# Eight of sixteen scale-and-add steps on the modulation row, moved from VectorE to POOL

## The chip, the cores and the metric

The kernel runs on one core of one Trainium2 chip. Its time is the device time of one execution in microseconds (us). TensorE is called PE here, ScalarE ACT, VectorE DVE, GpSimd POOL, and SyncE SP (in this kernel SP issues the weight loads). Each engine runs its own instruction list in order, and they meet at semaphores.

## The reference, cut to what matters

Two transformer-like blocks run one after the other on 256 tokens of width 2048, in float32. The change lies in the first block, where a condition vector `c` makes six modulation rows:

```
c_act = jax.nn.silu(c)
mod = c_act @ w_ada[l] + b_ada[l]
sh_m, sc_m, gt_m, sh_f, sc_f, gt_f = jnp.split(mod[:, None, :], N_MOD, axis=-1)
h = rmsnorm(x, pre_mix_norm[l]) * (1.0 + sc_m) + sh_m
proj = h @ w_in[l]
o_hg = hgrn2_group(proj[..., :HG_COLS], lb_all[l], hg_norm[l])
o_gdn = gdn_group(proj[..., HG_COLS:], gdn_conv_w[l], gdn_a_log[l], gdn_dt_bias[l], gdn_norm[l])
y = jnp.concatenate([o_hg, o_gdn], axis=-1) @ w_out[l]
x = x + gt_m * rmsnorm(y, post_mix_norm[l])
h = rmsnorm(x, pre_ffn_norm[l]) * (1.0 + sc_f) + sh_f
```

`sc_f` is the row of this change. It is a product of a vector of 2048 with 2048 columns of `w_ada`, and is first needed when `h` of the feed-forward is made. The two mixers, `hgrn2_group` (a decayed attention of 8 heads) and `gdn_group` (a gated delta rule with a triangular solve), stand between the projection `w_in` and the projection `w_out`.

## The kernel before

**Weights.** SP loads raw weights, 1 MB at a time (two k tiles of 128 rows by 1024 columns), into a ring of four slots, `raw_weights` (RAW). ACT rounds each k tile into `weights_high` (L351), DVE subtracts to get `weights_low` (L364), both in rings of four, and PE makes three products for each pair (L406 to L408). A load may start only when the user of the slot four loads before has said that it is done.

**The modulation rows.** `w_ada` goes through the same ring. A row of 2048 columns is summed in place, on all 128 partitions: for each k tile of 128 rows, `MOD = MOD + RAW * COLS[:, 112 + kt]`, where the last factor is one scalar of each partition. Later PE sums over the partitions with a matrix of ones (L1692). For `sc_f`, which lies in `MOD[:, 2, :]`, there are KT = 16 such steps, one 1 MB load each. Each is one DVE instruction on 128x2048 elements, recorded under L382 (`ada_step`, called by `ada_mix`). It counts up `ada_used`, on which the load four places later waits (L318). PE waits for all of them only in the first `w_out` chunk (`pe_mod2`, L1734). The first `w_out` chunk loads its first two pairs, then the sixteen `w_ada` tiles, then the rest.

**The mixers.** They run between the fourth k tile of the first `w_out` chunk and its fifth. Two programs are interleaved by hand, by strings of letters (L1521 to L1523): "h" is a step of the hgrn2 decay (class `Decay`), "g" one of the delta rule (`dve_delta`), "a" a modulation step, "n" the norm of the hgrn2 heads, "w" the weight of the delta rule's gate. In the DVE's list the order is:

1. Before the decay: two L364 of `w_out`, eight scalings (L1495), sixteen running sums along the tokens (L1503, a scan of 128x128 elements that has two SBUF inputs, the ones and the logs).
2. The decay, fourteen rounds of four instructions: two products (L992, L993), a difference (L985), and a masked copy of the scores from PSUM (L1001). At its end come two products (L1026, L1027).
3. The delta rule: the gram matrices (L1442 to L1455), then six levels of the triangular solve, each ended by two masked copies (L1461), then the addition L1464 and the outputs (L1467). The a, n and w steps stand between these.

**POOL.** It does little here. It clears a tile with a memset (L1548), then waits for the fifteenth decay (`decay_decays`) and copies the unit matrix twice into `XT` (L1551). The second gram step of DVE waits for that (`inverse_begun`). After that it makes two reciprocal roots (L621).

Of the kernel before, what the change touches and what calls it, by code (L numbers as in the profile page):

```python
# [11 lines left out]
F32 = mybir.dt.float32  # L12
F32R = mybir.dt.float32r
U8 = mybir.dt.uint8
ALU = mybir.AluOpType
# [127 lines left out]
def block_pair(nc, a, out, stop=None):  # L143

    with ExitStack() as ctx:
# [630 lines left out]
        def dve_first(dve):  # L776
# [32 lines left out]
            def input_low(q):  # L809
                k0, nk = GROUPS[q]  # L810
                for k in range(k0, k0 + nk):
                    dve.wait_ge(S("h_high"), k + 1)
                    dve.tensor_tensor(LL[:, k, :], XTURN[:, k, :], LH[:, k, :].bitcast(F32), ALU.subtract).then_inc(
                        S("h_low"), 1)

            dve.memset(STG[:, :, :], 0.0).then_inc(S("staged"), 1)
            dve.wait_ge(S("columns_ready"), 1)
# [552 lines left out]
        ADA_IN = 4 * KT  # L1370
        MIX_LOAD = MIX1.load_of(1) + 1

        def ada_mix(dve, first, count):

            for kt in range(first, first + count):
                m = MIX_LOAD + kt
                dve.wait_ge(S(f"weights_in{m % RAWN}"), 16 * (m // RAWN + 1))
                ada_step(dve, MOD[:, 2, :], RAW[:, m % RAWN, :, :].rearrange("p j n -> p (j n)"), kt, ADA_IN + kt)
# [104 lines left out]
                yield  # L1483

        def dve_ada_steps(dve):
            for kt in range(KT):
                ada_mix(dve, kt, 1)
                yield

# [30 lines left out]

        PE_PLAN = "g" + "h" * 6 + "g" + "h" * 14 + "g" * 4  # L1521
        ACT_PLAN = "hhh" + "g" + "hhh" + "g" + "h" * 12 + "g" + "r" + "gg" + "r" + "gg" + "r"
        DVE_PLAN = "hhhhg" + "h" * 27 + "g" + "aaa" + "ggg" + "a" + "nn" + "g" + "na" + "g" + "naa" + "gaaw" * 2 + "gaaa" + "gaa"  # L1523

        def dve_gdn_scale(dve):
            dve_rstd(dve, "gdn_heads", stat=STAT, n=DH)
# [19 lines left out]
        def pool_mix1(pool):  # L1546
            pool.wait_ge(S("hg_turned"), 1)
            pool.memset(PA[:, :, :], 0.0).then_inc(S("decay_cleared"), 1)  # L1548
            pool.wait_ge(S("decay_decays"), HG.TOTAL["decays"])
            for t in range(TT):  # L1550
                last = pool.tensor_copy(heads3(XT, t), IDENT.unsqueeze(1).to_broadcast([128, H1, 128]))  # L1551
            last.then_inc(S("inverse_begun"), 1)
            pool_rstd(pool, "hg_heads", STAT)
            pool_rstd(pool, "gdn_heads", STAT)
            pool.memset(MOD[:, 3, :], 0.0).then_inc(S("cleared"), 1)
            pool.wait_ge(S("cleared"), 2)
            pool.dma_start(MOD[0:1, 3, :], a["b_ada"][5 * D:6 * D].rearrange("(o n) -> o n", o=1)).then_inc(S("masks_in"), 16)
# [1223 lines left out]
```

## Time and profile before

| what | value |
|---|---|
| median of 3 runs | 2913.33 us (2912.28 to 2916.59) |
| span of the profiled execution | 2909.8 us |
| PE busy | 2702.3 us (93%) |
| DVE busy | 1819.0 us (63%) |
| ACT busy | 1224.1 us (42%) |
| POOL busy | 63.7 us (2%) |

The profile gives the span from the first to the last instruction of one execution. The median of the runs is 3.5 us above that span, and the profiled execution's own full time is not given apart from it. Busy shares are means over stages with different limits. In most of the program PE is what is waited for; the mixers, from about 476 us to about 645 us, are a stage of their own, and in it the share of the whole span says nothing.

In the rows further down a timeline's columns are: start in us, duration in us (of a merged group, from the start of its first to the end of its last), engine, line, operation, output<-inputs, how many, and in brackets the idle time before it with what ended it.

### The profile page before, as it was taken

To read this page: it belongs to the slowest core of one execution; us is meant where nothing else is said; L and a number is where in the kernel's file an instruction comes from. 1 tells how busy PE (TensorE), PEld (TensorE's weight loads), DVE (VectorE), ACT (ScalarE), POOL (GpSimd) and SP (SyncE) were. 2 spreads that over 40 slices of the span, in tenths; PEclk is the share of its full clock that TensorE was granted. 3 is DMA by queue.
4 is the path that set the end of the run, shared out by engine and by line. 5 is a ranking of instruction groups with operands and counts; after the bars stand their busy time and mean duration, and the time that the engine had idled before them with its cause. 6 is when DMAs were issued, how large, how long until landed. Compare 5 with 4: busy or idle time off the path is not lost.

```text
span 2909.8 us, 32548 instructions
## 1 busy us (share of the span) xinstructions
PE 2702.3 (93%) x12554; PEld 2188.7 (75%) x12554; DVE 1819.0 (63%) x2206; ACT 1224.1 (42%) x1560; POOL 63.7 (2%) x86
## 2 busy tenths in 40 slices
PE   4899998789799999999979999989999999999987
PEld 2378887687678888888767777877778887888876
DVE  7688677986865555555663556676455564646455
ACT  2134545333444444444444445444544434444333
POOL 1000000001000000000001000000000000000000
PEclk9899999999899999999989999999999999999998
DMA  9967885146575555555735443534345655465542
GB/s 377 338 213 268 289 313 192 58 174 249 209 259 185 186 188 190 187 185 187 259 117 199 148 141 131 187 118 173 132 172 175 201 174 195 167 201 174 165 154 100
DMA packets 154719, 562.29 MB, mean 193 GB/s; under 512 B 9688, under 2 KB 13943, under 8 KB 150768
## 3 DMA queue, kind: packets, MB, share of 16 engines
q1 hardware_dynamic: 150480, 542.15, 54.7%
q0 software_dynamic: 3952, 18.22, 1.8%
q8 instruction: 74, 1.21, 0.2%
q10 hardware_dynamic: 176, 0.40, 0.0%
q14 instruction: 37, 0.30, 0.0%
HBM read 556.28 MB, written 4.46 MB: 193 GB/s over the span
## 4 chain that ended last, share of the span: by engine, by line
PE 52%; issue 29%; DVE 12%; DMA 3%; ACT 3%; POOL 0%; DVEq 0%; SPq 0%; POOLq 0%; ACTq 0%
PE banks L406 15%; PE banks L408 15%; PE banks L407 15%; DMA raw_weights<-in_w_ada 3%; DVE weights_low L364 2%; ACT weights_high L351 2%; DVE mod_in L797 1%; PE banks L474 1%; DVE modulation L382 1%; PE banks L712 1%; DVE proj L1135 1%; DVE proj L1001 1%; PE banks L1692 0%; POOL small L621 0%; DVE proj L985 0%
## 5 line engine op out<-in xcount | busy, mean ns | idle before, releaser
L364 DVE TENSOR_TENSOR weights_low<-raw_weights,weights_high 128x1024 fp32r<-128x1024 f32 (+2 forms) x846 | 989.1, 1178 | 906.3 <-ACT weights_high L351 886.0
L351 ACT ACTIVATE weights_high<-raw_weights 128x1024 fp32r<-128x1024 f32 (+2 forms) x846 | 858.0, 1021 | 1018.2 <-PE banks L408 965.4
L406 PE MATMUL banks<-weights_high,lhs_high 128*128 128x512 f32 (+1 forms) x2208 | 883.7, 400 | 30.3 <-DVE weights_low L364 19.7
L408 PE MATMUL banks<-weights_high,lhs_low 128*128 128x512 f32 (+1 forms) x2208 | 865.4, 392 | 0.0
L407 PE MATMUL banks<-weights_low,lhs_high 128*128 128x512 f32 (+1 forms) x2208 | 864.6, 392 | 0.0
L406 PEld LDWEIGHTS banks<-weights_high,lhs_high 128*128 128x128 f32 x2208 | 420.1, 190 | 125.8 <-DVE weights_low L364 21.3
L408 PEld LDWEIGHTS banks<-weights_high,lhs_low 128*128 128x128 f32 x2208 | 419.5, 190 | 87.8
L407 PEld LDWEIGHTS banks<-weights_low,lhs_high 128*128 128x128 f32 x2208 | 420.5, 190 | 81.0 <-issue 1.0
L406 PE MATMUL banks<-weights_high,hid_high 128*128 128x512 f32 x856 | 337.5, 394 | 17.2 <-DVE hid_low L2563 6.4
L407 PE MATMUL banks<-weights_low,hid_high 128*128 128x512 f32 x856 | 335.2, 392 | 0.0
L408 PE MATMUL banks<-weights_high,hid_low 128*128 128x512 f32 x856 | 334.9, 391 | 0.0
L406 PEld LDWEIGHTS banks<-weights_high,hid_high 128*128 128x128 f32 x856 | 161.9, 189 | 57.4 <-DVE hid_low L2563 6.6
L408 PEld LDWEIGHTS banks<-weights_high,hid_low 128*128 128x128 f32 x856 | 162.0, 189 | 34.1
L407 PEld LDWEIGHTS banks<-weights_low,hid_high 128*128 128x128 f32 x856 | 162.1, 189 | 33.2 <-issue 0.2
L382 DVE SCALAR_TENSOR_TENSOR modulation<-raw_weights,columns,modulation 128x1024 f32<-128x1024 f32 (+1 forms) x112 | 160.6, 1434 | 2.6
L712 PE MATMUL banks<-first_weights,x_turned 128*128 128x512 f32 x192 | 93.6, 651 | 14.9 <-ACT x_turned L749 9.5
L797 DVE SCALAR_TENSOR_TENSOR mod_in<-raw_weights,columns,mod_in 128x512 f32<-128x512 f32 x120 | 89.1, 751 | 22.3 <-DMA raw_weights<-in_w_ada 18.2
L712 PEld LDWEIGHTS banks<-first_weights,x_turned 128*128 128x128 f32 x192 | 39.8, 211 | 65.7 <-issue 55.8
L2559 ACT ACTIVATE modulation<-modulation 128x512 f32<-128x512 f32 (+1 forms) x22 | 13.7, 622 | 107.9 <-DVE modulation L2586 107.9
L406 PE MATMUL banks<-weights_high,proj_turned 128*128 128x512 f32 x128 | 52.8, 413 | 4.2 <-DVE proj_turned L2232 2.5
L407 PE MATMUL banks<-weights_low,proj_turned 128*128 128x512 f32 x128 | 51.9, 406 | 0.0
L408 PE MATMUL banks<-weights_high,proj_turned 128*128 128x512 f32 x128 | 50.9, 398 | 0.0
(409 smaller groups left out, 2012.8 us busy)
## 6 DMA issues: line engine op xcount, KB each, us to landing
raw_weights<-in_w_ff SPq DMA_DIRECT2D x128, 1024.0 KB, 5.0
raw_weights<-in_w_ada SPq DMA_DIRECT2D x96, 1024.0 KB, 6.6
raw_weights<-in_w_in SPq DMA_DIRECT2D x96, 1024.0 KB, 5.4
raw_weights<-in_w_up SPq DMA_DIRECT2D x80, 1024.0 KB, 4.9
raw_weights<-in_w_down SPq DMA_DIRECT2D x42, 1024.0 KB, 5.1
raw_weights<-in_w_out SPq DMA_DIRECT2D x32, 1024.0 KB, 5.2
first_weights<-in_w_in SPq DMA_DIRECT2D x16, 768.0 KB, 12.6
raw_weights<-in_w_ckv SPq DMA_DIRECT2D x8, 1024.0 KB, 4.9
```

The lines of the kernel that those rows point to most:

```text
L351: act.activation(WHI[:, u % SPN, 0:c.width], RAW[:, n % RAWN, k % 2, 0:c.width], ACT.Copy).then_inc(S("high_made"), 1)
L364: dve.tensor_tensor(WLO[:, u % SPN, 0:c.width], RAW[:, n % RAWN, k % 2, 0:c.width], WHI[:, u % SPN, 0:c.width].bitcast(F32), ALU.subtract) ...
L382: dve.scalar_tensor_tensor(out=acc, in0=row, scalar=COLS[:, 112 + kt:113 + kt], in1=acc, op0=ALU.mult, op1=ALU.add).then_inc(S("ada_used"), 1)
L406: nc.tensor.matmul(o, x, hi, start=(k == 0), stop=False)
L407: nc.tensor.matmul(o, x, lo, start=False, stop=False)
L408: mm = nc.tensor.matmul(o, y, hi, start=False, stop=(k == c.kn - 1))
L474: tr = nc.tensor.transpose(bank[:, k, 128 * t:128 * t + 128], rows[:, t, c0:c0 + 128], IDENT)
L712: mm = nc.tensor.matmul(PS[:, bank, :], XTURN[:, k, 128 * t:128 * t + 128], raw[:, 512 * h:512 * h + 512], start=(k == 0), stop=(k == KT - 1))
L797: ins = dve.scalar_tensor_tensor(out=acc, in0=row, scalar=c, in1=acc, op0=ALU.mult, op1=ALU.add)
L1001: dve.copy_predicated(self.at[:, t, :].rearrange("p (h n) -> p h n", h=H), mask, self.slot(t).rearrange("p (h n) -> p h n", h=H)).then_inc ...
L1135: last = dve.scalar_tensor_tensor(out=dst, in0=src, scalar=w, in1=dst, op0=ALU.mult, op1=ALU.add)
L2559: act.activation(dst[:, 2 * q:2 * q + nk, :], GT[:, 2 * q:2 * q + nk, :], func).then_inc(S(done), 1)
```

## The change

POOL gets a function `pool_ada` with eight of the sixteen steps (kt 0 to 7). [...] POOL runs them after the memset and before the wait for the decays, and so before the two copies of the unit matrix. DVE keeps kt 8 to 15, and its order string is written anew. The count `h_low`, on which nothing waited, goes.

```
@@ -810,8 +810,7 @@
                 for k in range(k0, k0 + nk):
                     dve.wait_ge(S("h_high"), k + 1)
-                    dve.tensor_tensor(LL[:, k, :], XTURN[:, k, :], LH[:, k, :].bitcast(F32), ALU.subtract).then_inc(
-                        S("h_low"), 1)
+                    dve.tensor_tensor(LL[:, k, :], XTURN[:, k, :], LH[:, k, :].bitcast(F32), ALU.subtract)
@@ -1370,6 +1369,19 @@
         ADA_IN = 4 * KT
         MIX_LOAD = MIX1.load_of(1) + 1
 
+        POOL_STEPS = 8
+
+        def pool_ada(pool):
+
+            for kt in range(POOL_STEPS):
+                m = MIX_LOAD + kt
+                row = RAW[:, m % RAWN, :, :].rearrange("p j n -> p (j n)")
+                pool.wait_ge(S(f"weights_in{m % RAWN}"), 16 * (m // RAWN + 1))
+                pool.tensor_scalar(row, row, COLS[:, 112 + kt:113 + kt], None, ALU.mult).then_inc(S("row_scaled"), 1)
+                pool.wait_ge(S("row_scaled"), kt + 1)
+                pool.wait_ge(S("ada_used"), ADA_IN + kt)
+                pool.tensor_tensor(MOD[:, 2, :], MOD[:, 2, :], row, ALU.add).then_inc(S("ada_used"), 1)
+
@@ -1483,7 +1495,7 @@
         def dve_ada_steps(dve):
-            for kt in range(KT):
+            for kt in range(POOL_STEPS, KT):
                 ada_mix(dve, kt, 1)
                 yield
@@ -1520,7 +1532,7 @@
-        DVE_PLAN = "hhhhg" + "h" * 27 + "g" + "aaa" + "ggg" + "a" + "nn" + "g" + "na" + "g" + "naa" + "gaaw" * 2 + "gaaa" + "gaa"
+        DVE_PLAN = "hhhhg" + "h" * 27 + "gggg" + "nn" + "gn" * 2 + "gaw" * 2 + "gaaa" + "gaaa"
@@ -1546,6 +1558,7 @@
             pool.memset(PA[:, :, :], 0.0).then_inc(S("decay_cleared"), 1)
+            pool_ada(pool)
             pool.wait_ge(S("decay_decays"), HG.TOTAL["decays"])
```

Line numbers of the changed kernel are 12 or 13 higher in the mixers and 1 lower in the decay. Only two engines' lists differ. First POOL's, at the start of the mixers (`proj` is the tile that is cleared, `scratch` holds `XT`), in the kernel before:

```order
L1548 MEMSET proj 128x2x1024 [waits hg_turned]
L1551 COPY scratch<-tables 128x1024 [waits decay_decays]
L1551 COPY scratch<-tables 128x1024
L621 TENSOR_TENSOR small<-small 128x16 [waits mean_ready] x2
L1555 MEMSET modulation 128x2048
```

And in the changed kernel, the first three of the eight steps (the others are the same but for the slot):

```order
L1560 MEMSET proj 128x2x1024 [waits hg_turned]
L1380 TENSOR_SCALAR raw_weights<-raw_weights,columns 128x2048 [waits weights_in2]
L1383 TENSOR_TENSOR modulation<-modulation,raw_weights 128x2048 [waits ada_used,row_scaled]
L1380 TENSOR_SCALAR raw_weights<-raw_weights,columns 128x2048 [waits weights_in3]
L1383 TENSOR_TENSOR modulation<-modulation,raw_weights 128x2048 [waits ada_used,row_scaled]
L1380 TENSOR_SCALAR raw_weights<-raw_weights,columns 128x2048 [waits weights_in0]
L1383 TENSOR_TENSOR modulation<-modulation,raw_weights 128x2048 [waits ada_used,row_scaled]
```

Sixteen instructions of 128x2048 now stand between the memset and the copies.

Then DVE's list from the gram matrices to the first level of the solve, before:

```order
L1442 SCALAR_TENSOR_TENSOR scratch<-banks,modulation 128x1024
L1445 COPY_PREDICATED scratch<-masks,scratch 128x1024
L382 SCALAR_TENSOR_TENSOR modulation<-raw_weights,columns,modulation 128x2048 x3
L1442 SCALAR_TENSOR_TENSOR scratch<-banks,modulation 128x1024
L1445 COPY_PREDICATED scratch<-masks,scratch 128x1024
L1449 TENSOR_TENSOR modulation<-modulation,banks 128x1024 x2
L1452 SCALAR_TENSOR_TENSOR scratch<-banks,scratch 128x1024
L1455 TENSOR_TENSOR scratch<-scratch,banks 128x1024
L382 SCALAR_TENSOR_TENSOR modulation<-raw_weights,columns,modulation 128x2048
```

In the changed kernel:

```order
L1454 SCALAR_TENSOR_TENSOR scratch<-banks,modulation 128x1024
L1457 COPY_PREDICATED scratch<-masks,scratch 128x1024
L1454 SCALAR_TENSOR_TENSOR scratch<-banks,modulation 128x1024
L1457 COPY_PREDICATED scratch<-masks,scratch 128x1024
L1461 TENSOR_TENSOR modulation<-modulation,banks 128x1024 x2
L1464 SCALAR_TENSOR_TENSOR scratch<-banks,scratch 128x1024
L1467 TENSOR_TENSOR scratch<-scratch,banks 128x1024
```

All four modulation steps of that piece are gone. Last, DVE's list from the third level of the solve to the addition behind the sixth, before:

```order
L1461 COPY_PREDICATED proj<-masks,banks 128x1024 x2
L382 SCALAR_TENSOR_TENSOR modulation<-raw_weights,columns,modulation 128x2048 x2
L1481 TENSOR_TENSOR proj<-proj,small_rows 128x1024
L1461 COPY_PREDICATED proj<-masks,banks 128x1024 x2
L382 SCALAR_TENSOR_TENSOR modulation<-raw_weights,columns,modulation 128x2048 x2
L1481 TENSOR_TENSOR proj<-proj,small_rows 128x1024
L1461 COPY_PREDICATED proj<-masks,banks 128x1024 x2
L382 SCALAR_TENSOR_TENSOR modulation<-raw_weights,columns,modulation 128x2048 x3
L1461 COPY_PREDICATED scratch<-masks,banks 128x1024 x2
L382 SCALAR_TENSOR_TENSOR modulation<-raw_weights,columns,modulation 128x2048 x2
L1464 TENSOR_TENSOR proj<-proj,banks 128x1024
```

In the changed kernel:

```order
L1473 COPY_PREDICATED proj<-masks,banks 128x1024 x2
L382 SCALAR_TENSOR_TENSOR modulation<-raw_weights,columns,modulation 128x2048
L1493 TENSOR_TENSOR proj<-proj,small_rows 128x1024
L1473 COPY_PREDICATED proj<-masks,banks 128x1024 x2
L382 SCALAR_TENSOR_TENSOR modulation<-raw_weights,columns,modulation 128x2048
L1493 TENSOR_TENSOR proj<-proj,small_rows 128x1024
L1473 COPY_PREDICATED proj<-masks,banks 128x1024 x2
L382 SCALAR_TENSOR_TENSOR modulation<-raw_weights,columns,modulation 128x2048 x3
L1473 COPY_PREDICATED scratch<-masks,banks 128x1024 x2
L382 SCALAR_TENSOR_TENSOR modulation<-raw_weights,columns,modulation 128x2048 x3
L1476 TENSOR_TENSOR proj<-proj,banks 128x1024
```

Two levels have one step less, and behind the last level there is one more than before, three instead of two, ahead of the addition.

## Rows read from the trace of the kernel before

**Rows 1.** Busy time by stretch (us: PE, PEld, DVE, ACT, POOL; clock, DMA share, GB/s).

```profile
486.00:548.00 62.00, 36.85 (x273) 34.02 (x273) 60.67 (x64) 23.23 (x46) 3.01 (x2) 0.92 0.00 1
...
588.00:633.00 45.00, 40.57 (x351) 38.89 (x349) 41.00 (x25) 17.40 (x17) 0.00 (x0) 1.00 0.66 246
```

**Rows 2.** The chain of waits, 440 to 700 us: start, us, what.

```profile
480.48 5.17 DVE scratch L1503 x16
...
632.76 1.23 DVE proj L1464
```

**Rows 3.** DVE timeline, one round of the decay.

```profile
510.00 0.69 DVE L992 TENSOR_TENSOR proj<-proj,scratch 128x512 f32<-128x512 f32 x1
510.61 0.69 DVE L993 TENSOR_TENSOR scratch<-scratch 128x512 f32<-128x512 f32 x1
511.21 1.22 DVE L985 TENSOR_TENSOR proj<-scratch 128x1024 f32<-128x1024 f32 x1
512.34 1.30 DVE L1001 COPY_PREDICATED proj<-masks,banks 128x1024 f32<-128x1024 uint8 x1
```

**Rows 4.** Timeline of DVE and POOL at the end of the decay.

```profile
540.37 1.22 DVE L1019 TENSOR_TENSOR scratch<-scratch 128x1024 f32<-128x1024 f32 x1
...
543.71 3.01 POOL L1551 COPY scratch<-tables 128x1024 f32<-128x1024 f32 x2 [85.97 <-ACT proj L971]
543.88 1.95 DVE L1026 TENSOR_TENSOR scratch<-scratch 128x1024 f32<-128x1024 f32 x1
545.75 2.05 DVE L1027 TENSOR_TENSOR proj<-proj,scratch 128x1024 f32<-128x1024 f32 x1
```

**Rows 5.** The two POOL copies by themselves: duration in ns, least/median/most.

```profile
L1551 POOL COPY scratch<-tables x2: 1033/1528/2024, 543.7 to 544.7; 128x1024 f32<-128x1024 f32 x2
```

**Rows 6.** POOL's memset, and DVE beside it, timelines.

```profile
455.94 1.81 POOL L1548 MEMSET proj<- 128x2048 f32 x1 [350.92 <-PE banks L1150]
...
456.46 2.60 DVE L382 SCALAR_TENSOR_TENSOR modulation<-raw_weights,columns,modulation 128x1024 f32<-128x1024 f32 x2
```

**Rows 7.** POOL timeline: a two-input instruction, a power.

```profile
576.28 2.94 POOL L621 TENSOR_TENSOR small<-small 128x16 f32<-128x16 f32 x1 [29.56 <-DVE small L1040]
```

**Rows 8.** SP's issue of the first tile, and issues 455 to 640 us (last: us to landing).

```profile
463.79 0.34 SPq L320 DMA_DIRECT2D raw_weights<-in_w_ada  x1
...
raw_weights<-in_w_ada SPq DMA_DIRECT2D x16, 1024.0 KB, 5.0
```

**Rows 9.** DVE timeline ahead of the decay.

```profile
470.69 1.23 DVE L364 TENSOR_TENSOR weights_low<-raw_weights,weights_high 128x1024 fp32r<-128x1024 f32 x1 [1.50 <-ACT weights_high L351]
473.83 1.23 DVE L364 TENSOR_TENSOR weights_low<-raw_weights,weights_high 128x1024 fp32r<-128x1024 f32 x1 [1.92 <-ACT weights_high L351]
477.02 2.67 DVE L1495 TENSOR_SCALAR scratch<-scratch,small,columns 128x256 f32<-128x256 f32 x8 [1.97 <-ACT scratch L1354]
480.48 5.16 DVE L1503 TENSOR_TENSOR_SCAN scratch<-tables,scratch 128x128 f32<-128x128 f32 x16 [0.78 <-ACT scratch L1358]
```

**Rows 10.** DVE timeline, modulation steps in the delta rule and what waits beside them.

```profile
550.16 7.25 DVE L382 SCALAR_TENSOR_TENSOR modulation<-raw_weights,columns,modulation 128x2048 f32<-128x2048 f32 x3
560.26 1.22 DVE L1442 SCALAR_TENSOR_TENSOR scratch<-banks,modulation 128x1024 f32<-128x1024 f32 x1 [2.85 <-PE banks L1240]
...
568.99 2.34 DVE L382 SCALAR_TENSOR_TENSOR modulation<-raw_weights,columns,modulation 128x2048 f32<-128x2048 f32 x1
...
583.99 2.35 DVE L382 SCALAR_TENSOR_TENSOR modulation<-raw_weights,columns,modulation 128x2048 f32<-128x2048 f32 x1
...
627.35 4.79 DVE L382 SCALAR_TENSOR_TENSOR modulation<-raw_weights,columns,modulation 128x2048 f32<-128x2048 f32 x2
632.76 1.22 DVE L1464 TENSOR_TENSOR proj<-proj,banks 128x1024 f32<-128x1024 f32 x1 [0.62 <-PE banks L1279]
```

**Rows 11.** PE timeline in the solve, and ACT's first weight tile behind the mixers.

```profile
587.61 2.28 PE L1272 MATMUL banks<-tables,proj 128*128 128x128 f32 x16 [0.52 <-DVE proj L1461]
...
647.98 1.06 ACT L351 ACTIVATE weights_high<-raw_weights 128x1024 fp32r<-128x1024 f32 x1 [2.44 <-PE banks L408]
```

## The prediction

> **What bounds the kernel now.** I read the busy time by stretch first. From 486 to 548 us, the decay, DVE is busy 60.67 of 62 us; in the solve, 588 to 633 us, PE (40.57 of 45) and DVE (41.00) are both near full [rows 1]. The chain of waits then says which of them is waited for. It runs through DVE's sixteen scans at 480.48, and much later through the addition L1464 at 632.76 [rows 2]. DVE's timeline shows the decay as a closed row: L992, L993, L985 and L1001 start 0.61, 0.60 and 1.13 us apart, and the round ends at 513.64, 3.64 us after it began [rows 3]. No idle time stands in it. So the reader should see two regimes. Up to 548 us whatever delays DVE delays the end, one for one. Behind that the modulation steps on DVE fill time in which it would mostly wait for PE.
>
> The change takes work out of the second regime and puts work on POOL beside the first. The question is whether POOL's work is free there.
>
> **Does POOL hold DVE up?** The trace has one place where POOL reads SBUF while DVE does the same. L1019, a DVE instruction of 128x1024 with two SBUF inputs, takes 1.22 us alone. L1026 and L1027, of the same size and kind, take 1.95 and 2.05 us, and beside them run POOL's two copies [rows 4]. The first copy takes 1033 ns, from 543.71 to 544.74; the second, from 544.70, takes 2024 [rows 5]. Laid on one line: L1026 starts at 543.88 and ends at 545.83, which is 1.09 behind the end of copy 1. Copy 2 ends at 546.72, 0.89 behind the end of L1026. L1027 ends at 547.80, 1.08 behind the end of copy 2. That isn't two engines slowing each other a little. It is strict turns: each waits for the other's whole instruction, and the one that has waited goes next. DVE lost 0.73 + 0.83 us.
>
> The other place shows what doesn't collide: while POOL's memset of 2048 elements runs (455.94 to 457.75), two DVE steps L382 of 128x1024, also with two SBUF inputs, take 2.60 us together [rows 6]. Held to the memset's end they would have ended at 460.2 and not at 459.06. A memset reads nothing.
>
> The Trainium skill has the rule (SBUF — State Buffer, "Who interferes with whom"): a DVE instruction with two SBUF inputs contends with a GpSimd instruction that reads SBUF but not with one that only writes, and the loser blocks for the whole instruction. The trace agrees in both halves, by the 1.95 and 2.05 us and by the memset. It speaks against this change: both of POOL's new instructions read SBUF.
>
> **What a POOL step costs.** No row has POOL scaling or adding. Scaling reads one tile, as the copy does: 1.03 us for 1024 elements [rows 5], so 2.0 for 2048; memset's 1.81 [rows 6] is the end below. The addition reads two tiles. Its low end is the copy's rate, 2.0. If both inputs come through the door for which the copy took turns, it is twice that, 4.0. The only two-input row is a power, 2.94 us for 16 elements [rows 7], which by its rate would make 376 us of 2048; the power itself must cost that, since a copy goes through 1024 elements in 1.03, so it is no price of an addition. For a slow software loop I keep half as much again as high end, 3.0 and 6.0. I take 2.0 and 4.0, 6.0 us of held door per step.
>
> The Trainium skill (GPSIMD Engine Reference, section 3.1) has a measured 4497 ns for an fp32 tensor_tensor of 2048 elements. With it the total below would be 3.3 us more, about 2957 us. No run here shows it yet.
>
> **When, and beside what.** POOL is free from 457.75. The first tile's load is issued at 463.79 and takes 5.0 us to land [rows 8], so POOL starts at about 469 to 469.5. The next tiles come ahead of need: a slot is given back at each addition's end, its load takes 5.0, and it is wanted three steps, 18 us, later. From there, in turns with DVE [rows 9]:
> - Scaling 0 from 469.5 to 471.5; the L364 due at 470.69 (1.14 us) goes next; addition 0 from 472.6 to 476.6, and the L364 of 473.83 is pushed to 477.8. The eight scalings L1495 read one tile (2.67 us), run freely, and end near 480.5, when the scans start anyway. Cost so far nothing.
> - Scaling 1 follows that L364, 477.8 to 479.8, and addition 1 runs from 480.1 to 484.1. The scans, due at 480.48, have two SBUF inputs: 3.6 us lost.
> - Six steps are left, twelve instructions. Between each two goes one scan of 0.32 us (5.16/16). DVE loses 6 x 6.0 = 36.0 us.
>
> The sum is 39.6 us, and the scans stretch from 5.2 to about 45. POOL is done at about 524, before the decay is, so the fourteen rounds then run at 3.64 us again, and POOL's copies still come in time for `inverse_begun`. PE and ACT only wait longer. DVE is the chain there, so nothing gives this back.
>
> **What DVE gains and loses later.** The three steps at 550.16 (7.25 us) go, but DVE idled 2.85 us behind them for a PE product [rows 10]: worth nothing. The steps at 568.99 and 583.99 stand ahead of L1461 of the first two levels; the row of PE behind the second shows 0.52 idle on L1461 [rows 11], so I take 0.5 us gained, where 0 and 4.7 (both steps in full) are the ends. In the levels after that, PE's products of one level hide one or two steps. Behind the sixth level there are now three steps, not two: 627.35 plus 7.2 (the three at 550.16 took 7.25) is 634.5, but L1464 was wanted and started at 632.76, after 0.62 idle [rows 10], and is on the chain [rows 2]. That is 1.7 us lost. The last tiles of `w_out` are loaded up to 2.5 us later; ACT took the first of them at 647.98 after waiting for PE, not for a load [rows 11]: nothing. The missing count `h_low` costs nothing, since no one waits for it.
>
> **The sum.** +39.6 - 0.5 + 1.7 = +40.8 us. The profiled span was 2909.8; 2950.6 is the span after. The median of the runs stands 3.5 us above the span, so 2954 us.
>
> **The rivals.**
> 1. *The scans don't take turns*, only the products do. For it: no row shows a scan beside a reading POOL. Against: it has two SBUF inputs as L1026 has. POOL then runs three more instructions freely, and in the decay 1.2 us of L1001 (which reads PSUM and the masks) hides part of each third instruction: played through in the same way, 26 us lost, 2941 us. An addition at the copy's rate gives 24 us, 2938. I call both the small case, 2930 to 2946.
> 2. *POOL is slow.* With 3.0 and 6.0 us a step is 9.0: 6 x 9.0 plus 6 ahead, +60, 2974 us; above 2968 I count this case. If POOL is so slow or so often last that it ends after 543.7, the delay shows at L1551 and L1442 instead, of the same size.
> 3. *Not slower: POOL's work passes beside DVE's*, as the memset did [rows 6]. This would be so if only copies from the constant tables collide, or if POOL's two-input loop lets DVE in between elements. It is decided at L992 and L985: if they stay at 0.69 and 1.22 beside POOL, the price is zero. Then only the late terms are left: +1.2, or 2914.5 us; with both early steps on the chain in full, 4.7 - 1.7 = 3.0 gained, 2910. Against it stand L1026 and L1027. A form between, where DVE loses 6 to 16 us, gives 2920 to 2930.
> 4. *The relief counts for more than I read.* DVE sheds eight steps of 2.34 us [rows 10], 18.7 in all, and some of it might shorten levels that look bound by PE. Beside a POOL that collides with nothing, that is the only way to be faster. PE's 40.57 of 45 us [rows 1] leaves at most 4 us there, so 2906.
>
> **How the numbers follow.** Forecast, 2946 to 2968: 0.58. Small case: 0.16. Slow POOL: 0.11. Between, 2920 to 2930: 0.05. Nothing held, 2910 to 2919: 0.06. Relief: 0.04. What a measurement can tell from no change is about 0.2%, 5.8 us. Slower is 0.58 + 0.16 + 0.11 + 0.05 = 0.90; same 0.06; faster 0.04. The range from 2930 to 2980 takes in the forecast, the small case and most of the slow one, and leaves out 0.15 below and about 0.05 above.
>
> **What would show it.** Right: the group of scans takes about 45 us instead of 5.16, in pieces between POOL's instructions; POOL's sixteen instructions end near 524; rounds of the decay behind that keep 3.64 us; the decay's end moves from 547.80 to about 587; L1464 (now L1476) starts with no idle before it, and the distance from L1027's end to it grows from 85.0 to about 86.2 us. Wrong: two-input DVE instructions beside POOL at their old lengths, scans at 0.32 us each while POOL adds, or a gram step that waits for POOL's copies.

## The result, and the profile after

| what | before | changed |
|---|---|---|
| median in one comparison | 2914.96 us (2912.28 to 2917.97, 4 runs) | 2971.25 us (2970.3 to 2973.13, 4 runs) |
| span of the profiled execution | 2909.8 us | 2969.7 us |
| DVE busy | 1819.0 us | 1863.3 us |
| POOL busy | 63.7 us | 145.5 us |

The ratio is 1.0189 [1.0175, 1.0203]: slower by 56.3 us. The forecast was 2954, so the direction was right and the size 17 us too small: the result lies inside the stated range of 2930 to 2980, but above the 2946 to 2968 of the forecast, in the case of a slow POOL. DVE gave eight instructions of 2.34 us away and is busy for 44 us more, which by itself says that something else holds it.

The kernel after, timelines of POOL and of DVE at the start of the mixers (start, us, engine, line, what).

```profile
457.38 1.81 POOL L1560 MEMSET proj<- 128x2048 f32 x1 [352.08 <-PE banks L1149]
471.36 5.45 POOL L1380 TENSOR_SCALAR raw_weights<-raw_weights,columns 128x2048 f32<-128x2048 f32 x1 [12.17 <-DMA raw_weights<-in_w_ada]
476.90 4.77 POOL L1383 TENSOR_TENSOR modulation<-modulation,raw_weights 128x2048 f32<-128x2048 f32 x1
481.66 5.47 POOL L1380 TENSOR_SCALAR raw_weights<-raw_weights,columns 128x2048 f32<-128x2048 f32 x1
487.21 4.49 POOL L1383 TENSOR_TENSOR modulation<-modulation,raw_weights 128x2048 f32<-128x2048 f32 x1
...
548.78 4.88 POOL L1383 TENSOR_TENSOR modulation<-modulation,raw_weights 128x2048 f32<-128x2048 f32 x1
602.23 3.01 POOL L1564 COPY scratch<-tables 128x1024 f32<-128x1024 f32 x2 [48.57 <-ACT proj L970]
```

```profile
472.13 5.16 DVE L364 TENSOR_TENSOR weights_low<-raw_weights,weights_high 128x1024 fp32r<-128x1024 f32 x2 [1.49 <-ACT weights_high L351]
478.46 38.89 DVE L1507 TENSOR_SCALAR scratch<-scratch,small,columns 128x256 f32<-128x256 f32 x8 [1.17 <-ACT scratch L1353]
517.39 20.61 DVE L1515 TENSOR_TENSOR_SCAN scratch<-tables,scratch 128x128 f32<-128x128 f32 x16
538.13 0.06 DVE L1519 MEMSET small<- 128x1 f32 x1
538.13 5.26 DVE L984 TENSOR_TENSOR proj<-scratch 128x1024 f32<-128x1024 f32 x1
...
604.26 2.05 DVE L1026 TENSOR_TENSOR proj<-proj,scratch 128x1024 f32<-128x1024 f32 x1
```

The line numbers shift: the decay's L992, L993, L985 and L1001 are now L991, L992, L984 and L1000, and the last two products L1026 and L1027 are now L1025 and L1026. Against [rows 9] and [rows 4] the reader sees three places. The eight scalings (L1495 before, L1507 now) take 38.89 us instead of 2.67, the sixteen scans 20.61 instead of 5.16, and the products of the decay are held until POOL ends at 553.66. The next views put their durations side by side (ns: least, median, most); the first row is of the kernel before.

```profile
L1495 DVE TENSOR_SCALAR scratch<-scratch,small,columns x8: 407/408/412, 477.0 to 479.3; 128x256 f32<-128x256 f32 x8
```

```profile
L1507 DVE TENSOR_SCALAR scratch<-scratch,small,columns x8: 3358/5092/5528, 478.5 to 511.8; 128x256 f32<-128x256 f32 x8
L1515 DVE TENSOR_TENSOR_SCAN scratch<-tables,scratch x16: 391/393/4676, 517.4 to 537.6; 128x128 f32<-128x128 f32 x16
L1380 POOL TENSOR_SCALAR raw_weights<-raw_weights,columns x8: 5448/5474/6410, 471.4 to 542.3; 128x2048 f32<-128x2048 f32 x8
L1383 POOL TENSOR_TENSOR modulation<-modulation,raw_weights x8: 4492/4568/4881, 476.9 to 548.8; 128x2048 f32<-128x2048 f32 x8
```

A POOL step is 5.47 + 4.49 = 10.0 us where the forecast had 2.0 + 4.0. Exactly eight POOL instructions, the addition at 476.90 to the scaling at 511.73, stand beside the eight scalings of DVE: one of DVE's goes between each two, in strict turns.

The windows show who waits for it (columns as in [rows 1]).

```profile
478.00:538.00 60.00, 7.17 (x48) 7.01 (x48) 59.50 (x24) 8.79 (x12) 59.50 (x13) 0.56 0.36 123
538.00:606.00 68.00, 41.08 (x272) 38.26 (x272) 67.50 (x64) 23.30 (x46) 18.59 (x5) 0.85 0.09 31
606.00:621.00 15.00, 13.43 (x85) 13.16 (x86) 3.10 (x4) 5.02 (x11) 0.00 (x0) 0.69 0.00 1
```

From 478 to 538 us DVE and POOL are both busy all the time, with 24 DVE instructions that need 7.83 us between them in [rows 9], and PE has 7.17 us of work. Nothing fills this stretch, so it is added to the span.

The loss in pieces, each as the distance between two starts after, less the same before: from the first scaling to the first scan 38.93 - 3.46 = 35.5 us, over the scans 20.74 - 5.29 = 15.4, over the decay 66.13 - 59.98 = 6.2. That is 57.1 us, where the forecast had 39.6, all of it at the scans. The border between scans and decay is a DVE memset; in the kernel before it is this row:

```profile
485.77 0.06 DVE L1507 MEMSET small<- 128x1 f32 x1
```

Outside the 57.1 us, the first scaling starts 1.4 us later than before (478.46 and 477.02); POOL's memset, ahead of POOL's new work, starts 1.44 later too. That is no effect of the change: in another trace, of a kernel whose list is the same as before up to there (the last experiment), that memset starts at 457.18, 1.24 later. The rest is in the delta rule, below.

### The profile page after: what moved, and what is told of

Same layout as the page of the kernel before. It is cut to its first block, busy times and chain, and to the rows that moved or that the text cites. A ratio compares the mean times of both kernels' runs of the same rounds, so it can differ in the third digit from the quotient of the medians.

```text
span 2969.7 us, 32557 instructions
## 1 busy us (share of the span) xinstructions
PE 2712.1 (91%) x12554; PEld 2198.2 (74%) x12554; DVE 1863.3 (63%) x2198; ACT 1224.3 (41%) x1560; POOL 145.5 (5%) x102
## 4 chain that ended last, share of the span: by engine, by line
PE 52%; issue 28%; DVE 13%; ACT 3%; DMA 3%; POOL 0%; SPq 0%; DVEq 0%; POOLq 0%; ACTq 0%
PE banks L406 15%; PE banks L408 15%; PE banks L407 15%; DMA raw_weights<-in_w_ada 3%; DVE weights_low L364 2%; ACT weights_high L351 2%; DVE mod_in L797 1%; DVE scratch L1507 1%; PE banks L712 1%; DVE modulation L382 1%; PE banks L474 1%; DVE scratch L1515 1%; DVE proj L1134 1%; DVE proj L984 1%; PE banks L1264 1%
## 5 line engine op out<-in xcount | busy, mean ns | idle before, releaser
L382 DVE SCALAR_TENSOR_TENSOR modulation<-raw_weights,columns,modulation 128x1024 f32<-128x1024 f32 (+1 forms) x104 | 141.8, 1364 | 2.1
L621 POOL TENSOR_TENSOR small<-small 128x1 f32<-128x1 f32 (+3 forms) x17 | 15.9, 935 | 1254.3 <-DVE small L606 1009.2
L406 PE MATMUL banks<-weights_high,proj_turned 128*128 128x512 f32 x128 | 52.8, 413 | 4.2 <-DVE proj_turned L2245 2.5
L928 PE MATMUL banks<-scratch 128*128 128x128 f32 x32 | 6.4, 391 | 52.5 <-DVE small L1519 52.5
## 6 DMA issues: line engine op xcount, KB each, us to landing
first_weights<-in_w_in SPq DMA_DIRECT2D x16, 768.0 KB, 12.6
```

Of the source, the lines that this page charges most:

```text
L382: dve.scalar_tensor_tensor(out=acc, in0=row, scalar=COLS[:, 112 + kt:113 + kt], in1=acc, op0=ALU.mult, op1=ALU.add).then_inc(S("ada_used"), 1)
L406: nc.tensor.matmul(o, x, hi, start=(k == 0), stop=False)
```

## The experiments

Diffs are against the changed kernel. The time of the profiled execution stands about 1.8 us above its span here. A time with a ratio is a median of 4 to 10 runs; one without is a single run, and single runs of the kernel before lie between 2909 and 2919 us, so a few us between two such times say nothing. A steadier measure, which also leaves out what comes behind the decay, is the start of the decay's last instruction (L1026; L1027 in the kernel before), counted from the start of POOL's memset ahead of the mixers. In the kernel before and in the three kernels that have no such work on POOL ahead of L1026 it agrees within 0.05 us.

| kernel | POOL's memset | L1026 | distance | above the kernel before |
|---|---|---|---|---|
| before | 455.94 | 545.75 | 89.81 | |
| changed | 457.38 | 604.26 | 146.88 | 57.1 |
| count only | 457.84 | 547.68 | 89.84 | 0.0 |
| additions only | 456.48 | 576.01 | 119.53 | 29.7 |
| four steps on POOL | 457.77 | 578.51 | 120.74 | 30.9 |
| only writes on POOL | 458.18 | 560.61 | 102.43 | 12.6 |
| DVE's scalings by constants | 457.32 | 598.73 | 141.41 | 51.6 |
| POOL scales by a constant | 458.52 | 604.04 | 145.52 | 55.7 |
| POOL scales by a repeated column | 456.80 | 602.38 | 145.58 | 55.8 |
| POOL's steps behind the scans | 455.68 | 598.73 | 143.05 | 53.2 |
| the same, repeated column | 456.61 | 597.11 | 140.50 | 50.7 |
| the same, copy | 457.04 | 585.71 | 128.67 | 38.9 |
| three steps, behind POOL's copies | 456.95 | 546.81 | 89.86 | 0.0 |
| four of DVE's steps in the gap | 457.18 | 547.02 | 89.84 | 0.0 |

**Count only.** POOL's steps are left out; a memset of one column does the counting. The eight steps' part of the sum is missing.

```
-                pool.tensor_scalar(row, row, COLS[:, 112 + kt:113 + kt], None, ALU.mult).then_inc(S("row_scaled"), 1)
-                pool.wait_ge(S("row_scaled"), kt + 1)
                 pool.wait_ge(S("ada_used"), ADA_IN + kt)
-                pool.tensor_tensor(MOD[:, 2, :], MOD[:, 2, :], row, ALU.add).then_inc(S("ada_used"), 1)
+                pool.memset(SM[:, 220:221], 0.0).then_inc(S("ada_used"), 1)
```

> Leaves POOL's eight scalings and eight additions out (a one-column memset counts in their place), and keeps DVE's new order. Turns theory (DVE waits for POOL's whole instructions): nothing of that is left, only the late terms of the order, +1.2 us, so 2914 to 2918. Rival (the new DVE order or later loads cost much by themselves): well above, 2930 or more.

Measured: 2916.39 us, ratio 1.0006 [0.9996, 1.0015]. L1026 starts as far behind the memset as in the kernel before. So the whole loss comes from what POOL executes; eight steps fewer on DVE, in another order, give nothing that the runs can tell. This also takes the rival of the relief away.

**Additions only.** The scaling is left out.

```
-                pool.tensor_scalar(row, row, COLS[:, 112 + kt:113 + kt], None, ALU.mult).then_inc(S("row_scaled"), 1)
-                pool.wait_ge(S("row_scaled"), kt + 1)
```

> Leaves the scaling out; POOL only adds the raw tile. Turns theory: POOL's addition stays 4.5 us, the loss is the sum of POOL's instructions from 478.5 us on, some 2.5 + 6 x 4.5 = 30 us, plus 1.2: about 2945. Rival (the loss goes by the number of collisions or by something else than the length): it would stay near 2971, or halve its 57 to about 2943; the row of one DVE scaling beside an addition tells these apart (4.6 us each under turns).

Measured: 2939.54 us, below both 2943 and 2945, so the time alone does not part them; the scalings do, with 4662 ns in the median against the 4.6 us of the turns theory. DVE's timeline of this kernel:

```profile
480.65 28.30 DVE L1505 TENSOR_SCALAR scratch<-scratch,small,columns 128x256 f32<-128x256 f32 x8
508.98 5.16 DVE L1513 TENSOR_TENSOR_SCAN scratch<-tables,scratch 128x128 f32<-128x128 f32 x16
```

The scans are untouched, since POOL is done at 508.8 us. The scalings pay most: 28.30 us for 2.67 us of work. Of the 29.7 us, 24.9 lie between the first scaling and the first scan. Another 3.1 lie ahead of them, and 1.8 in the decay, where the first masked copy waits 2.78 us for PE instead of 1.05 (PE's granted clock was 0.73 in the first 15 us of the decay, 0.91 in the kernel before).

**Four steps on POOL.** DVE has the other twelve, in an order close to that of the kernel before.

```
-        POOL_STEPS = 8
+        POOL_STEPS = 4
-        DVE_PLAN = "hhhhg" + "h" * 27 + "gggg" + "nn" + "gn" * 2 + "gaw" * 2 + "gaaa" + "gaaa"
+        DVE_PLAN = "hhhhg" + "h" * 27 + "gggg" + "a" + "nn" + "g" + "na" + "g" + "na" + "gaaw" * 2 + "gaaa" + "gaa"
```

> POOL does four steps, DVE twelve. Turns theory: four steps of 10 us less on DVE's path, so 57 - 40 = 17 us lost and about 2932. Rival (a fixed cost of having POOL at work there, or of the clock): more than half of the 57 stays, 2943 or more.

Measured: 2941.61 us, just under the rival's 2943 and 10 us above the forecast. DVE's timeline:

```profile
478.86 32.98 DVE L1507 TENSOR_SCALAR scratch<-scratch,small,columns 128x256 f32<-128x256 f32 x8 [1.97 <-ACT scratch L1353]
511.87 5.16 DVE L1515 TENSOR_TENSOR_SCAN scratch<-tables,scratch 128x128 f32<-128x128 f32 x16
```

Half the steps cost about half (30.9 of 57.1 us), so a fixed cost is not what one sees. Nearly all of it, 29.6 us, is paid by eight instructions that in the prediction ran free. My expectation took off 10 us for each step left out. The four that are left out are the ones that fall beside the scans and the decay, where a step costs less, as a later experiment shows.

**Only writes on POOL.** Each of the sixteen instructions becomes a memset of the raw tile; the sums are left out.

```
-                pool.tensor_scalar(row, row, COLS[:, 112 + kt:113 + kt], None, ALU.mult).then_inc(S("row_scaled"), 1)
+                pool.memset(row, 0.0).then_inc(S("row_scaled"), 1)
-                pool.tensor_tensor(MOD[:, 2, :], MOD[:, 2, :], row, ALU.add).then_inc(S("ada_used"), 1)
+                pool.memset(row, 0.0).then_inc(S("ada_used"), 1)
```

> Each of POOL's sixteen instructions is replaced by a memset of the same tile (1.81 us), which only writes; the eight steps' sums are left out. If only POOL's reads collide, neither scalings nor scans are held: 2915. If an instruction of DVE that uses both ports for one tile also needs POOL's write side, the eight scalings take about 1.8 to 2 us each beside the memsets and the scans stay at 0.32: about 8 x 1.8 = 14 us more, 2929.

Measured: 2925.46 us, nearest to the second of the two cases. The durations of the scalings, then the times of the two engines:

```profile
L1507 DVE TENSOR_SCALAR scratch<-scratch,small,columns x8: 1258/1966/1971, 479.3 to 491.8; 128x256 f32<-128x256 f32 x8
```

```profile
479.27 14.48 DVE L1507 TENSOR_SCALAR scratch<-scratch,small,columns 128x256 f32<-128x256 f32 x8 [1.97 <-ACT scratch L1353]
493.79 5.16 DVE L1515 TENSOR_TENSOR_SCAN scratch<-tables,scratch 128x128 f32<-128x128 f32 x16
```

```profile
493.55 1.95 POOL L1380 MEMSET raw_weights<- 128x2048 f32 x1
495.55 1.80 POOL L1383 MEMSET raw_weights<- 128x2048 f32 x1
```

The two kinds of DVE instruction part here. A scaling with one SBUF input is held by a mere write, from 0.41 to 1.97 us. The scans, with two SBUF inputs, run beside POOL's memsets at their old length (5.16 us for the sixteen), as L382 did in [rows 6]. The Trainium skill (SBUF — State Buffer, "Who interferes with whom") says why the first can be: tensor_scalar may enter a mode that uses both port pairs, its own and the one shared with GpSimd. In the prediction I weighed the sentence of that section on two-input instructions and passed over this one; this run agrees with it, by the 1.97 us.

**DVE's scalings by constants.** The two scalars of each partition become -0.5 and 0.5.

```
-                last = dve.tensor_scalar(Lb[1][:, :, hs], Lb[2][:, :, hs], LB_LESS_1[:, h:h + 1], COLS[:, 104 + h:105 + h],
+                last = dve.tensor_scalar(Lb[1][:, :, hs], Lb[2][:, :, hs], -0.5, 0.5,
```

> The eight DVE scalings ahead of the scans take constants and not two scalars per partition. If the scalars' reads made them wait for POOL, they now take 0.4 us each beside POOL, and the scans take the turns in their place, so the time stays within 3 us of 2971. If they wait because the instruction uses both ports for its one tile, they still take about 5 us each; time 2971 as well.

Measured: 2968.21 us. The eight take 18.60 us and not 38.89, the longest of them 5449 ns, about a whole scaling of POOL:

```profile
L1507 DVE TENSOR_SCALAR scratch<-scratch x8: 273/1425/5449, 478.4 to 496.7; 128x256 f32<-128x256 f32 x8
497.04 20.53 DVE L1515 TENSOR_TENSOR_SCAN scratch<-tables,scratch 128x128 f32<-128x128 f32 x16
```

Neither forecast fits. Four of the eight are still held (2.57, 5.45, 4.58 and 5.45 us), so the reading of scalars is not what holds them; but behind each of these one passes in about 0.3 us. So here DVE does two instructions between two of POOL's, and not one. Why is open. Of the 20 us saved here all but 5.5 come back, since POOL's other steps then fall beside the decay.

**POOL scales by a constant.** In POOL's scaling the scalar of each partition becomes 0.5.

```
-                pool.tensor_scalar(row, row, COLS[:, 112 + kt:113 + kt], None, ALU.mult).then_inc(S("row_scaled"), 1)
+                pool.tensor_scalar(row, row, 0.5, None, ALU.mult).then_inc(S("row_scaled"), 1)
```

> The scaling is by the constant 0.5 and not by the condition's column. If the scalar read for each partition makes it 5.47 us, it falls to about 2.0 and the time to about 2971 - 7 x 3.5 = 2947. If POOL's tensor_scalar is slow whatever the scalar, 5.4 us and 2971.

Measured: 2973.55 us, the second case; POOL's scaling takes 5435 ns in the median, against 5474. The scalar's source is not the price.

**POOL scales by a repeated column.** The scaling becomes a multiplication of two tiles, one of which is the column repeated.

```
-                pool.tensor_scalar(row, row, COLS[:, 112 + kt:113 + kt], None, ALU.mult).then_inc(S("row_scaled"), 1)
+                pool.tensor_tensor(row, row, COLS[:, 112 + kt:113 + kt].to_broadcast([128, 2 * UW]), ALU.mult).then_inc(
+                    S("row_scaled"), 1)
```

> The scaling is made by tensor_tensor with the scalar's column repeated along the tile, as two inputs. If POOL's tensor_scalar of 5.47 us is slow because of its own code, this one costs 4.5 like the addition: seven steps of 1.0 us less, 2964. If every multiplication costs 5.4 on POOL, no change, 2971.

Measured: 2970.73 us, ratio 1.0192 [1.0175, 1.0209]. That is the time of the rival, but not for its reason, since the multiplication does not cost 5.4 us. The scaling is shorter by a third and the kernel no faster:

```profile
L1380 POOL TENSOR_TENSOR raw_weights<-raw_weights,columns x8: 3646/3680/4578, 469.5 to 529.0; 128x2048 f32<-128x2048 f32 x8
512.80 27.91 DVE L1516 TENSOR_TENSOR_SCAN scratch<-tables,scratch 128x128 f32<-128x128 f32 x16
```

What the scalings of DVE save (32.79 us instead of 38.89) the scans pay (27.91 instead of 20.61). That asked for a finer look at what of POOL's scaling holds DVE.

**POOL's steps behind the scans.** POOL waits for the memset that ends the scans, so all its steps fall on the decay.

```
             pool.memset(PA[:, :, :], 0.0).then_inc(S("decay_cleared"), 1)
+            pool.wait_ge(S("decay_inputs"), 1)
             pool_ada(pool)
```

> POOL's steps wait until the scans are done and run beside the decay rounds only. Turns theory: sixteen instructions of 80 us in all, one DVE instruction with two SBUF inputs between each two, hidden only behind the masked copies (1.2 us of each third): about +74 in the decay, 2990. Rival (POOL slows DVE in proportion to its traffic, wherever it runs): the same 57 as before, 2971.

Measured: 2969.34 us. My expectation of 2990 was 21 us too high, and the rival's 2971 was right in the number. The round of the decay tells why. DVE, then POOL:

```profile
504.04 4.49 DVE L991 TENSOR_TENSOR proj<-proj,scratch 128x512 f32<-128x512 f32 x1
508.45 0.68 DVE L992 TENSOR_TENSOR scratch<-scratch 128x512 f32<-128x512 f32 x1
509.06 4.65 DVE L984 TENSOR_TENSOR proj<-scratch 128x1024 f32<-128x1024 f32 x1
513.63 1.30 DVE L1000 COPY_PREDICATED proj<-masks,banks 128x1024 f32<-128x1024 uint8 x1
515.00 4.49 DVE L991 TENSOR_TENSOR proj<-proj,scratch 128x512 f32<-128x512 f32 x1
```

```profile
503.48 4.50 POOL L1383 TENSOR_TENSOR modulation<-modulation,raw_weights 128x2048 f32<-128x2048 f32 x1
507.96 6.40 POOL L1380 TENSOR_SCALAR raw_weights<-raw_weights,columns 128x2048 f32<-128x2048 f32 x1
514.44 4.51 POOL L1383 TENSOR_TENSOR modulation<-modulation,raw_weights 128x2048 f32<-128x2048 f32 x1
```

One POOL step goes with one round of DVE, 10.96 us from 504.04 to 515.00 instead of the 3.64 of [rows 3]: 7.3 us lost per step. The addition costs L991 4.49 - 0.69 = 3.8. POOL's scaling costs L984 only 4.65 - 1.22 = 3.4, and it still runs for 0.65 us after L984 has ended at 513.71. L984 needs 1.22 us, so it was let in at about 512.5, some 1.9 us before the scaling's end at 514.36. The masked copy, with its data in PSUM, keeps 1.30. L992 keeps 0.68: it passes while the scaling has only begun, and the scaling in turn takes 6.40 us here and not 5.47. So the rival's reason fails: a POOL that slowed DVE in proportion to its traffic would stretch all four instructions.

The theory from this: POOL's tensor_scalar of 5.47 us holds a two-input DVE instruction for some 3.6 us, and not for a tail of about 1.8, in which it might only write, since a memset of the same tile takes 1.81. The scans of the changed kernel agree: one scan beside an addition, but many beside the end of a scaling (two answers of its timeline on DVE, each a stretch of one POOL instruction).

```profile
527.67 4.65 DVE L1515 TENSOR_TENSOR_SCAN scratch<-tables,scratch 128x128 f32<-128x128 f32 x1
532.24 5.44 DVE L1515 TENSOR_TENSOR_SCAN scratch<-tables,scratch 128x128 f32<-128x128 f32 x6
```

Two runs test it at the place where all of DVE's held instructions have two SBUF inputs. Both are the kernel with POOL's steps behind the scans, with another instruction in place of POOL's scaling. **The repeated column, behind the scans:**

```
-                pool.tensor_scalar(row, row, COLS[:, 112 + kt:113 + kt], None, ALU.mult).then_inc(S("row_scaled"), 1)
+                pool.tensor_tensor(row, row, COLS[:, 112 + kt:113 + kt].to_broadcast([128, 2 * UW]), ALU.mult).then_inc(
+                    S("row_scaled"), 1)
```

> As the run in which POOL's eight steps start behind the fill of decay_inputs (2969.3 us), and POOL's scaling is made by a multiplication with the repeated column, which took 3.65 us where it stood alone in place of 5.47. Theory, refined: only the part of a POOL instruction in which it still reads holds VectorE's instructions of two SBUF inputs; the scaling by tensor_scalar reads for about 3.65 us and only writes for the last 1.8. Then the shorter form gains nothing: it holds (3.65 + 4.5) x 8 = 65 us, less what falls beside the masked copies, 53 to 59 us lost, 2968 to 2975 us. Rival, POOL's instruction holds VectorE for its whole length: 8 steps get shorter by 1.8 to 2.7 us, 14 to 22 us in all, 2948 to 2955 us.

Measured: 2966.85 us. Against the kernel with tensor_scalar there, L1026 comes 143.05 - 140.50 = 2.5 us sooner, or 0.3 per step. The theory had none, and the rival 14 to 22. **A copy in place of the scaling, behind the scans** (the scaling is left out):

```
-                pool.tensor_scalar(row, row, COLS[:, 112 + kt:113 + kt], None, ALU.mult).then_inc(S("row_scaled"), 1)
+                pool.tensor_copy(row, row).then_inc(S("row_scaled"), 1)
```

> As the run in which POOL's eight steps start behind the fill of decay_inputs (2969.3 us), with the scaling left out and a copy of the raw row onto itself in its place, which by the copies of 128x1024 at 1.03 us takes about 2.0 us. Theory, refined (what POOL reads holds VectorE): (2.0 + 4.5) x 8 = 52 us, less some 6 beside masked copies, about 46 us lost, 2961 us. Rival, whole length: POOL's step falls from 10.96 to about 6.5 us, 8 x 4.4 = 35 us less than 2969, 2934 us.

Measured: 2953.19 us, L1026 at 585.71. The forecast of 2961 was 8 us too high and the rival's 2934 19 us too low. The difference to the tensor_scalar there is 143.05 - 128.67 = 14.4 us, or 1.8 per step. A tensor_scalar that holds for 3.65 and a copy that holds for 2.0 differ by 1.65; their whole lengths differ by about 3.5. The theory is the nearer one, not exact.

```profile
L1380 POOL TENSOR_TENSOR raw_weights<-raw_weights,columns x8: 4042/4048/4587, 486.6 to 551.7; 128x2048 f32<-128x2048 f32 x8
```

```profile
L1380 POOL COPY raw_weights<-raw_weights x8: 2337/2607/2888, 487.0 to 539.0; 128x2048 f32<-128x2048 f32 x8
```

(The first row is of the run with the column, the second of the run with the copy; both hold waits for DVE.) The tail of about 1.8 us shows in three places: at L984 here, at the scans, and at a masked copy in the next run. That it is a phase of writing is argued, not shown: from the memset's length, and from DVE's scalings, which a memset holds and which are also held to the end of POOL's scaling (5.1 to 5.5 us).

**Three steps, behind POOL's copies.** POOL makes three steps, where DVE waits for PE.

```
-        POOL_STEPS = 8
+        POOL_STEPS = 3
-        DVE_PLAN = "hhhhg" + "h" * 27 + "gggg" + "nn" + "gn" * 2 + "gaw" * 2 + "gaaa" + "gaaa"
+        DVE_PLAN = "hhhhg" + "h" * 27 + "gggg" + "nn" + "gna" + "gnaa" + "gaaa" + "gaaw" + "gaaa" + "gaaw"
-            pool_ada(pool)
             pool.wait_ge(S("decay_decays"), HG.TOTAL["decays"])
...
             last.then_inc(S("inverse_begun"), 1)
+            pool_ada(pool)
```

> POOL does three steps, behind its two copies of the unit matrix (about 547 to 577 us), where most of DVE's instructions read PSUM and DVE waits for PE; DVE does thirteen. Turns theory: held are only the masked copy from SBUF (L1457) and the two products of the hgrn2 heads, up to 5 us each and partly in idle time: 2917 to 2925. Rival (POOL's reading holds every DVE instruction): 30 us, 2944. If nothing is held, 2915.

Measured: 2921.15 us, against 2915.86 of the kernel before beside it, ratio 1.0014 [1.0002, 1.0027]. Timeline of DVE, then POOL's first scaling:

```profile
548.78 1.21 DVE L1454 SCALAR_TENSOR_TENSOR scratch<-banks,modulation 128x1024 f32<-128x1024 f32 x1
550.03 3.57 DVE L1457 COPY_PREDICATED scratch<-masks,scratch 128x1024 f32<-128x1024 uint8 x1
563.06 1.23 DVE L1454 SCALAR_TENSOR_TENSOR scratch<-banks,modulation 128x1024 f32<-128x1024 f32 x1 [9.47 <-PE banks L1239]
564.32 5.62 DVE L1457 COPY_PREDICATED scratch<-masks,scratch 128x1024 f32<-128x1024 uint8 x1
577.74 4.31 DVE L1032 TENSOR_TENSOR proj<-proj 128x1024 f32<-128x1024 f32 x2
```

```profile
547.77 6.40 POOL L1380 TENSOR_SCALAR raw_weights<-raw_weights,columns 128x2048 f32<-128x2048 f32 x1
```

The first masked copy needs 1.30 us and ends at 553.60, so it was let in at 552.30, 1.87 us before the scaling's end at 554.17: the tail again. It costs nothing, since DVE waits 9.47 us behind it. The second (L1457 at 564.32) and the third (L1032) are on the chain of waits. Three steps in the best gap I found still lose about 4 us (0.6 to 7.9 by the interval), against some 20 of three where the change has them (57.1/8 = 7.1 each).

**Four of DVE's steps in the gap.** This is the kernel before with one step moved from behind the gram matrices into the gap ahead of them, to see if the freed place was worth something.

```
-        DVE_PLAN = "hhhhg" + "h" * 27 + "g" + "aaa" + "ggg" + "a" + "nn" + "g" + "na" + "g" + "naa" + "gaaw" * 2 + "gaaa" + "gaa"
+        DVE_PLAN = "hhhhg" + "h" * 27 + "g" + "aaaa" + "ggg" + "nn" + "g" + "na" + "g" + "naa" + "gaaw" * 2 + "gaaa" + "gaa"
```

> The kernel before, with the fourth modulation step moved from behind the gram matrices into the gap of 2.85 us ahead of them, all on DVE. The gap holds it whole (2.3 us), and one step leaves the way of the solve's first level: 0.2 to 0.6 us gained in the profile, no difference that the runs can tell, 2913 to 2915.

Measured: 2916.38 us against 2915.86, ratio 0.9996 [0.9986, 1.0006]. No difference. From the second gram step to L1464 the trace has 71.94 us instead of 72.50, the 0.56 that was expected. No version that I ran beats the kernel before.

## Why the prediction was right in direction and short in size

1. *DVE is the chain in this stretch, one for one.* Right within 2 us. L1026 moved by 58.5 us (57.1 from POOL's memset on), L1476 by 61.6 and the span by 59.9.
2. *POOL's reads hold DVE in strict turns.* Right for an addition of POOL, which holds DVE to its end, and the rival of no turns on scans is out: a scan beside an addition took 4676 ns. "Not held" is out too. The decay's first product takes 4.49 us for 0.69 beside an addition, and its difference 4.65 for 1.22 beside a scaling. Not right for the whole of POOL's scaling, see 5. (The 460.2 in the passage on the memset should be 460.35, 457.75 + 2.60, which changes nothing there.)
3. *"The eight scalings L1495 read one tile (2.67 us), run freely."* Wrong. They took 38.89 us, 35.5 of the 57.1. A memset alone holds them, so one input does not make an instruction free; none of the rows that I had read shows POOL at work beside such a one. They gave eight short instructions, each to be held by one whole POOL instruction. But this moved the loss more than it made it: with POOL's steps behind the scans the scalings are free again, and the loss is still 53.2 us. The sum had charged most of POOL's work to the scans in their place.
4. *A step is 2.0 + 4.0.* This is the term that made the sum too small. The addition is 4.49, above the 4.0 that the copy's rate gave. It equals the 4497 ns of the Trainium skill (GPSIMD Engine Reference, section 3.1), with which the sum had been 2957. The scaling is 5.47, also above the 3.0 that I kept as its high end: it reads one tile as the copy does, and does not run at the copy's rate. With 10.0 in place of 6.0 the term of six steps alone would have been 60 us.
5. *What offset it.* Not in the prediction: the tail of POOL's scaling lets two-input instructions pass, so only 7.3 to 7.7 of 10.0 us per step are lost in the decay and the scans (two steps cost the scans 15.4 us). So the measured 57.1 lies under those 60. By its time and by its cause, dear POOL instructions, the result belongs to the rival of a slow POOL. That it comes so near that rival's 2974 is in part luck: its step of 9.0 us was too short, and it knew no tail.
6. *POOL is done near 524, the rounds behind it keep 3.64.* The first half is wrong: POOL ended at 553.66. The second half is right: L991 at 561.21 and 564.86 starts 3.65 apart. POOL's copies still came in time.
7. *The late terms, -0.5 and +1.7.* Right. From the second gram step (L1442, now L1454) to L1464 (now L1476) the distance grew from 72.50 to 73.68, by 1.2: up to the sixth level 0.57 less, behind it 1.75 more. L1476 starts with no idle before it:

```profile
684.71 2.56 DVE L1473 COPY_PREDICATED scratch<-masks,banks 128x1024 f32<-128x1024 uint8 x2
687.17 7.25 DVE L382 SCALAR_TENSOR_TENSOR modulation<-raw_weights,columns,modulation 128x2048 f32<-128x2048 f32 x3
694.33 1.22 DVE L1476 TENSOR_TENSOR proj<-proj,banks 128x1024 f32<-128x1024 f32 x1
```

8. *L1027's end to L1464 grows from 85.0 to 86.2.* It grew to 88.0. The extra 1.9 us lie between the decay's end and the second gram step (14.34 us against 12.46), where PE's granted clock was 0.69 (the third window above has the same) and 0.83 in the kernel before. It isn't the change: the kernel that only counts has 14.3 there as well (549.73 to 564.04), at 0.69, and the one with POOL's steps behind the scans 12.1 at 0.88. So it goes with how much of this stretch PE spends at the lower of its two clock levels. What decides that is not shown.
9. *The median 3.5 us above the span.* It was 1.6. In every later run the profiled execution's time is about 1.8 us above its span, so I estimate that the profiled execution of the kernel before was some 1.7 us quicker than the median (3.5 - 1.8). That is part of why the span grew by 59.9 us and the median by 56.3.

## What to carry to other kernels

An idle POOL is not free capacity beside a DVE that bounds the stage: most of each POOL instruction that reads SBUF is counted as DVE time, unless DVE's instructions beside it take their data from PSUM, or DVE waits anyway. Do not take a DVE instruction with a single SBUF input for free, and expect a short one to pay as much as a long one, the whole POOL instruction beside it. Price POOL's instructions by form, since a scaling and a copy of one tile differ by more than two to one, and ask what a shorter one would free: a scaling shorter by a third changed nothing, while three steps placed where DVE mostly waits cost about 4 us and not 20.

## What the runs showed of the hardware that I had not expected

- POOL on 128x2048 float32: tensor_scalar 5.47 us (5.44 with a constant), multiplication by a repeated column 3.65, addition of two tiles 4.49, memset 1.81.
- DVE's tensor_scalar of 128x256 from SBUF, 0.41 us alone, takes 1.97 beside memsets and 3.4 to 5.5 beside POOL's reads. Scans of 128x128 with two SBUF inputs pass memsets freely and are held by an addition for its whole length.
- POOL's tensor_scalar holds a two-input DVE instruction for about 3.6 of its 5.47 us; POOL's addition of two tiles holds one to its end (4.49 us for 0.69). A DVE tensor_scalar with scalars of each partition is held to its end.
- A masked copy is held when its data lies in SBUF (3.57 and 5.62 us for 1.30), and not when it lies in PSUM.
